# GpSimd's u product in four pieces, VectorE's mixer work in another order, and one down projection whose last k comes at the end

## The reference

```python
# first block: u and vs are gelu of columns of h @ w_in
mixed = einsum('gij,bnjgc->bnigc', masked(sg_w), blocks(layernorm(vs))) + sg_b
sgo = (u * mixed * silu(zs)) @ w_sg_out

# second block: 16 meta rows are put ahead, h has 528 rows
p_pool, p_bval, p_bgate, p_cgate, p_cx = split(rmsnorm(h) @ w_in_2)      # 256 256 256 512 512
y_a = pool_mixer(p_pool)                      # moving means of 2, 4, 8, 16 rows, then a small product
y_b = conformer_conv(p_bval, p_bgate)         # 31-tap causal convolution, layernorm, silu, small product
y_c = gelu(p_cgate) * rglru(p_cx)             # 4-tap convolution, two gates, a linear scan over rows
h = h + concat(y_a, y_b, y_c) @ w_out_2
h = h + square(relu(rmsnorm(h) @ w_up_2)) @ w_down_2
out = rmsnorm(h)[16:]
```

## Time and profile before

| | |
|---|---|
| median of 3 runs | 1053.14 us (1053.1 to 1058.57) |
| profiled execution, its time | 1053.21 us |
| its span | 1051.4 us |
| TensorE busy | 1028.8 us, 98% |
| VectorE, ScalarE, GpSimd busy | 515.1, 421.4, 575.9 us |

### The profile page before, as it was taken

The page is one execution under the profiler, slowest core; times in us unless marked ns, Lnnn a source line. Parts: engine busy times, 40 slices in busy tenths (PEclk is TensorE's granted clock), DMA queues, the critical chain, the costliest instruction groups (busy, mean ns, idle before and its releaser), DMA issues.

```text
span 1051.4 us, 12703 instructions
## 1 busy us (share of the span) xinstructions
PE 1028.8 (98%) x5047; PEld 861.9 (82%) x5047; DVE 515.1 (49%) x835; ACT 421.4 (40%) x663; POOL 575.9 (55%) x712
## 2 busy tenths in 40 slices
PE   9999999999999999999999878999999999999997
PEld 7888888888888888888899766888788888888887
DVE  2781356665356633545677898457113213312323
ACT  5443445555624424443237663453213222212332
POOL 3655556556556764465634796464655544554551
PEclk9999999999999999999999999999999999999999
DMA  6323222122442215332222202322323232232212
GB/s 223 105 92 93 89 70 81 54 67 81 141 140 80 80 45 181 118 120 82 81 80 81 80 21 81 101 81 80 120 80 112 89 110 91 87 113 81 97 64 80
DMA packets 93500, 98.63 MB, mean 94 GB/s; under 512 B 3282, under 2 KB 88816, under 8 KB 93440
## 3 DMA queue, kind: packets, MB, share of 16 engines
q1 hardware_dynamic: 93440, 97.81, 28.7%
HBM read 95.71 MB, written 2.10 MB: 93 GB/s over the span
## 4 chain that ended last, share of the span: by engine, by line
PE 84%; DVE 11%; ACT 4%; issue 1%; DMA 1%; SPq 0%; DVEq 0%; ACTq 0%
PE ps L347 75%; DVE ps L1165 2%; PE ps L714 1%; PE ps L695 1%; PE ps L1623 1%; PE ps L839 1%; DVE Fm L1077 1%; DVE Hl L478 1%; PE ps L652 1%; PE ps L654 1%; DVE tmp L1589 1%; DVE Fm L1129 1%; DMA raw<-in_w_in 1%; DVE tmp L456 1%; DVE Al L1531 1%
## 5 line engine op out<-in xcount | busy, mean ns | idle before, releaser
L268 POOL TENSOR_TENSOR wlo<-raw,whi 128x256 fp32r<-128x256 f32 x668 | 509.4, 794 | 386.1 <-ACT whi L263 386.1
L347 PE MATMUL ps<-Hh,whi 128*128 128x512 f32 x832 | 330.0, 397 | 5.4 <-DVE Hl L1246 1.7
L347 PE MATMUL ps<-Hl,whi 128*128 128x512 f32 x832 | 325.4, 391 | 0.0
L263 ACT ACTIVATE whi<-raw 128x1024 fp32r<-128x1024 f32 x167 | 175.9, 1054 | 159.0 <-PE ps L347 152.7
L347 PE MATMUL ps<-Hh,wlo 128*128 128x512 f32 x832 | 209.1, 390 | 1.0 <-POOL wlo L268 1.0
L347 PE MATMUL ps<-Ah,whi 128*128 128x512 f32 (+1 forms) x576 | 197.7, 366 | 0.2 <-DVE Al L1531 0.2
L347 PE MATMUL ps<-Al,whi 128*128 128x512 f32 (+1 forms) x576 | 195.0, 361 | 0.0
L347 PEld LDWEIGHTS ps<-Hh,whi 128*128 128x128 f32 x832 | 156.9, 189 | 42.7 <-DVE Hl L408 4.2
L347 PEld LDWEIGHTS ps<-Hh,wlo 128*128 128x128 f32 x832 | 156.6, 188 | 34.2 <-POOL wlo L268 1.4
L347 PEld LDWEIGHTS ps<-Hl,whi 128*128 128x128 f32 x832 | 156.9, 189 | 31.8 <-issue 0.5
L347 PE MATMUL ps<-Ah,wlo 128*128 128x512 f32 (+1 forms) x576 | 125.2, 363 | 0.0
(11 more groups left out here) (291 smaller groups left out, 957.2 us busy)
## 6 DMA issues: line engine op xcount, KB each, us to landing
raw<-in_w_in SPq DMA_DIRECT2D x33, 1024.0 KB, 5.3
raw<-in_w_up SPq DMA_DIRECT2D x16, 1024.0 KB, 5.4
raw<-in_w_down SPq DMA_DIRECT2D x16, 1024.0 KB, 5.1
raw<-in_w_att_out SPq DMA_DIRECT2D x4, 1024.0 KB, 5.2
raw<-in_w_sg_out SPq DMA_DIRECT2D x4, 1024.0 KB, 5.2
raw<-in_w_o SPq DMA_DIRECT2D x4, 1024.0 KB, 5.1
raw<-in_w_in SPq DMA_DIRECT2D x6, 512.0 KB, 3.9
Fm<-in_x SPq DMA_DIRECT2D x2, 1024.0 KB, 6.7
```

Source lines behind the costliest of these rows:

```text
L263: eh = A(lambda e, s=s, src=src, kk=kk: e.activation(wtile(whi, s, kk), src, ACT.Copy), raw_ev[b], used)
L268: el = G(lambda e, s=s, src=src, kk=kk, cut=cut: e.tensor_tensor(wtile(wlo, s, kk)[:, *cut], src[:, *cut], f(wtile(whi, s, kk))[:, *cut], ...
L347: return e.matmul(ps[:, bk, 0:c1 - c0], wt, x[:, k, c0:c1], start=st, stop=sp)
```

## The change

1. The u product of each `sg_block` is four GpSimd instructions of two groups of 128 columns instead of one of eight; all are queued together, and the last one signals.
2. `single` takes `tail`, and the first down product of each part gets `tail=1`: the high·high, low·high and high·low matmuls of k 0 to 6 come first, those of k = 7 at the end.
3. In `w_in_2` the two pool products come ahead of the four for `p_cgate`. In each half of `w_out_2` the product over k 0 and 1 comes first: W0, R0, R1, W1, R2, R3.
4. The steps of `mixers` are written anew. The side taps are put one channel at a time (`side_tap`), channel 0's from the fifth step on; the pool mixer comes ahead of the gating; the four gated tiles are handled one at a time, three of them left in their PSUM banks (`at_cg`) until their low half is made; taps stand between a copy's request and its use; `x1_add` comes in two parts behind R0 and R1.

The core of the diff, with the steps that the prediction speaks of:

```diff
+        cols("w_in_2", 0, 0, 1)
         cols("w_in_2", 0, 768, 2)
-        cols("w_in_2", 0, 0, 1)
         for i in range(2):
+            cols("w_out_2", 0, 512 * i, 1, 2, 1)
             cols("w_out_2", 512, 512 * i, 1, 4)
-            cols("w_out_2", 0, 512 * i, 1, 2, 1)
...
-            sg[("u", i)] = G(lambda e: e.tensor_tensor(u, u, t1.rearrange("p (g i) -> p g i", g=8), ALU.mult), e1,
-                             zu_ev[7])
+            t8 = t1.rearrange("p (g i) -> p g i", g=8)
+            for g in range(0, 8, 2):
+                u = F4[:, g:g + 2, 128 * i:128 * i + 128]
+                sg[("u", i)] = G(lambda e, g=g, u=u: e.tensor_tensor(u, u, t8[:, g:g + 2], ALU.mult), e1, zu_ev[7],
+                                 signal=(g == 6))
...
+        def at_cg(c):
+            return ps[:, order4[c], :] if c < 3 else cg[:, c]
...
+                ev = V(lambda e, c=c: e.tensor_tensor(Hl[:, 4 + c], at_cg(c), f(Hh[:, 4 + c]), ALU.subtract),
+                       cg_ev[c])
+                y2[4 + c] = [ev]
+                if c < 3:
+                    bank_free[order4[c]] = ev
...
             cx(3, *made[7])
+            side_tap(0)
             taps(1, (1,))
             rg_conv(3)
             rg_high(3)
+            taps(1, (1,))
             rg_low(3)
+            rg_scan(1)
+            yield
+            rg_gate(2, 0)
+            side_tap(1)
             yield
             rg_gate(2, 1)
+            pool_in(0, *made[8])
+            side_tap(0)
+            rg_input(2)
+            yield
+            rg_gate(3, 0)
+            e3 = pool_mix(0)
+            side_tap(1)
+            yield
+            rg_gate(3, 1)
+            pool_in(1, *made[9])
+            ea = pool_high(0, e3)
+            rg_exps(2)
+            rg_input(3)
+            es = pool_low(0, ea)
+            yield
+            e3 = pool_mix(1)
+            side_tap(1)
+            rg_root(2)
+            table(ACT.Gelu_apprx_tanh)
+            ea = pool_high(1, e3)
+            yield
             scale_cg(0)
+            es1 = pool_low(1, ea)
+            gelus((0,))
...
+            taps(3)
+            side_tap(1)
+            yield
             scale_cg(3)
             gelus((3,))
             taps(1)
+            cg_hi((3,))
             taps(1)
+            cg_lo((3,))
             yield
             taps(3)
             yield
             taps(3)
             yield
+            taps(3)
+            yield
+            x1_add((0, 1), rec_mm)
+            taps(3)
+            yield
+            taps(3)
+            yield
+            x1_add((2, 3), rec_mm)
             taps(N_DVE)
             merged = conv_merge()
...
         for h in range(2):
+            product([[(bk, 0, 512)] for bk in order4], Hh, Hl, y2, (0, 1), 2, last=False, mid=step)
+            step()
             for g in range(2):
-                product([[(order4[2 * g], 0, 512)], [(order4[2 * g + 1], 0, 512)]], Hh, Hl, y2, range(4, 8), 4, last=False, mid=step)
+                rec_mm.extend(product([[(order4[2 * g], 0, 512)], [(order4[2 * g + 1], 0, 512)]], Hh, Hl, y2,
+                                      range(4, 8), 4, first=False, last=(h == 0), mid=step))
                 step()
...
-                bk, em = single(Hh, Hl, acts, nb=nb)
+                bk, em = single(Hh, Hl, acts, nb=nb, tail=1 if n == 0 else 0)
```

More of the change, by code:

```diff
@@ L458, in scaled, with single @@
             return ev
-        def single(xh, xl, kev, ks=range(8), nb=4):
+        def single(xh, xl, kev, ks=range(8), nb=4, tail=0):
             bk = one_bank(nb)
-            return bk, product([[(bk, 0, 512)]], xh, xl, kev, ks)[0]
+            return bk, product([[(bk, 0, 512)]], xh, xl, kev, ks, tail=tail)[0]
         def h_product(nb=4):
@@ L1166, in taps, with side_tap @@
                         acc, ub[:, c, k:k + 512], cw[:, c, k:k + 1], acc, ALU.mult, ALU.add), tap_ev[c])
[L1168 to L1184, removed]
+        def side_tap(c):
+            k = side_at[c]
+            side_at[c] += 1
+            x = ub[:, c, k:k + 512]
+            s, fr = new_tmp()
+            dst = tmp[:, s, 0:512]
+            ea = A(lambda e: e.activation(dst, x, ACT.Copy, scale=cw[:, c, k:k + 1]), ub_ev[c], fr)
+            if k == N_DVE:
+                side_to[c], side_ev[c] = s, ea
+                return
+            acc = tmp[:, side_to[c], 0:512]
+            side_ev[c] = G(lambda e: e.tensor_tensor(acc, acc, dst, ALU.add), ea, side_ev[c])
+            release(s, side_ev[c])
@@ L1250, in conv_merge @@
         def conv_merge():
-            assert tap_at == [N_DVE, N_DVE] and side_at[0] == 31
+            assert tap_at == [N_DVE, N_DVE] and side_at == [31, 31]
             ev, ea = [], []
@@ L1354, in mixers @@
             rg_high(0)
+            taps(1, (0,))
             rg_low(0)
+            side_tap(0)
             yield
             rescale(5, 6)
+            side_tap(0)
             yield
@@ L1360, in mixers @@
             cx(1, *made[3])
-            taps(1, (0,))
+            taps(2, (0,))
             rg_conv(1)
             rg_high(1)
+            taps(1, (0,))
             rg_low(1)
@@ L1374, in mixers @@
             rg_gate(1, 1)
+            taps(2, (0,))
             rg_exps(0)
             rg_input(1)
-            taps(2, (0,))
             yield
             conv_input(1, *made[5])
+            taps(1, (0,))
             rg_root(0)
+            table(ACT.Sigmoid)
             yield
-            side_taps()
+            side_tap(0)
             taps(2, (0,))
             rg_scan(0)
-            table(ACT.Sigmoid)
             yield
             cx(2, *made[6])
-            rg_scan(1)
+            side_tap(0)
@@ L1389, in mixers @@
+            taps(1, (0,))
             rg_conv(2)
             rg_high(2)
+            taps(1, (0,))
             rg_low(2)
             yield
-            side_taps()
-            taps(1, (1,))
+            side_tap(0)
+            side_tap(1)
             yield
             cx(3, *made[7])
-            taps(1)
+            side_tap(0)
+            taps(1, (1,))
+            rg_conv(3)
+            rg_high(3)
+            taps(1, (1,))
+            rg_low(3)
+            rg_scan(1)
             yield
@@ L1421, in mixers @@
+            scale_cg(2)
+            gelus((2,))
             taps(1)
-            yield
[L1423 to L1430, removed]
+            cg_hi((2,))
+            pool_out_low(1, e5)
+            taps(1)
+            cg_lo((2,))
+            side_tap(1)
+            yield
+            taps(3)
+            side_tap(1)
             yield
@@ L1486, in build @@
             step()
+        for i in range(2):
+            made.append(pair_product(mid=step))
+            step()
         order4 = (2, 3, 0, 1) if max(bank_age[0:2]) > max(bank_age[2:4]) else (0, 1, 2, 3)
```

86 lines of the change are left out of this document (29 added, 57 removed).

## The result

The changed kernel takes 1047.07 us (median of six, 1045.33 to 1047.73), the kernel before 1054.86 beside it (six, 1052.78 to 1059.85): a ratio of 0.9915, 95% interval [0.9893, 0.9937]. That is faster, and inside the range. The forecast 1044.9 of 1053.21 is a ratio of 0.9921. The profiled execution took 1047.22, with a span of 1045.3. The kernel before's profiled execution, 1053.21, lies near the short end of its six, so between the two profiled executions the gain is only 6.0 us where 8.3 were forecast, and that the ratio comes so close to the forecast's is in part luck.

A forecast was written before the change was run, and what follows sets the result against it. TensorE, busy for 98% of the span, was taken as the bound, so only its waits could be won: 1053.21 - 6.5 (mixers) - 0.9 (spatial gate) - 0.95 (down product) = 1044.9 us, range 1040 to 1050.5.

The forecast's parts named there:

- The mechanism: Mixers: VectorE's last low half, at 634.2, holds TensorE at R0's seventh matmul; 66 matmuls, 15.0 us, follow to `conv_sums`.
- The mixers' term: Mixers: the new order starts `conv_sums` at 649.2 instead of 655.75, a gain of 6.5 us.
- I let that instruction start where it did: Mixers, VectorE: the third `cx` was assumed to start at 575.75, as in the kernel before.
- GpSimd's idle time: Mixers: channel 0's side-tap additions, four steps earlier, are covered by GpSimd's idle 14.5 of 79.9 us.
- The stretch from there to the last low half: VectorE, third `cx` to last low half: 54.1 us of work plus 4.3 of waits, the latter between 0 and 7.7.
- The gate (2, 1): Mixers: TensorE waits 3 to 4 us for a sigmoid queued behind tile 3's high half, without cost to the end.
- W0 was given some 6: Mixers: TensorE waits some 6 us at W0 for the second pool tile and gated tiles' banks, without cost to the end.
- The small edits: Spatial gate's u product in pieces gains 0.9 us; the first down product's tail gains 0.95 in part 0.
- The waits for ScalarE: Rival, mixers: idle time of 7.7 instead of 4.3 and one more lower-clock stretch give 1049.8 us; chance 0.25.
- The lower clock behind W0's wait: Rival, TensorE at W0: another lower-clock stretch costs 1.5 us, giving 1046.4; inside the forecast's own range, no separate chance.
- VectorE could be faster: Rival, mixers: taps fill every wait and `conv_sums` comes near TensorE's bound of 642.4; about 1040 us, chance 0.18.
- Pieces acting as one: Rival, spatial gate: the u product's four pieces act as one, giving 1045.8 us; inside the forecast's own range, no separate chance.

The follow-up runs named there:

- b4: Changed kernel without GpSimd's additions of the side taps (taps 23 to 30 missing from the convolution): 1043.48 us, one run.
- a4: Changed kernel with all four gated tiles in SBUF, none left in PSUM: 1048.3 us, one run.
- b1: Changed kernel with the high and low halves of recurrence tiles 1 and 3 a step later, so ScalarE has the gates' sigmoids first: 1046.76 us, one run.
- b2: Changed kernel with the second pool tile's high copy moved on ScalarE ahead of the square roots and table load: 1047.82 us, one run.
- b3: Changed kernel with the edits of b1 and b2 together: 1045.23 us, ratio 0.9899 to the kernel before.
- a1: Kernel before with only GpSimd's u product in four pieces: 1053.62 us, one run.
- a2: Kernel before with only the last k at the end of each part's first down product: 1052.07 us, one run.
- a3: Changed kernel with u product in one piece and down products as before, leaving only the new order: 1049.18 us, ratio 0.9933 to the kernel before.
- c1: b3 with each of GpSimd's side-tap additions in two pieces of 256 columns: 1044.5 us, ratio 0.9891 to the kernel before.
- d1: b3 with the second channel half's last four side taps moved behind the last low half: 1044.98 us, ratio 0.9898 to the kernel before.
- d2: b3 with the edits of c1 and d1 together: 1042.58 us, ratio 0.988 to the kernel before.
- e1: d2 with the second pool tile's product and evictions half a product earlier and k = 7 last in R0's first product: 1041.65 us, ratio 0.9856 to the kernel before.

## Why the prediction came out as it did

**The mechanism** was right for the changed kernel. VectorE's last low half sets `conv_sums`: TensorE waits for it at 635.78, and the 66 matmuls behind it take 15.1 us where 15.0 was worked out. When b4 brings it 2.8 us earlier, the sums follow by 2.8, though TensorE then comes 0.1 us behind it and has no wait left. In a4 it is the longer wait at W0, for an earlier low half of the same queue, and the lower clock behind it that hold TensorE.

**The mixers' term was mis-sized**: 4.3 us instead of 6.5. Of the missing 2.2, the step that failed most is "I let that instruction start where it did": the third `cx` comes 1.46 later. The traces show how. TensorE has a new wait of 1.47 us at gate (1, 0), for a sigmoid. From the end of gate (1, 1)'s matmuls, by way of the square roots, to the third `cx` it is 10.31 us in both kernels, so the shift lies ahead of that. On ScalarE that sigmoid stood behind the copy of tile 1's high half and a weight copy before, too, so the order there did not do it. The copy itself is later, because the three instructions of `rg_conv(1)` ahead of it on VectorE are longer. They are, in the kernel before and then in the changed one, with a GpSimd addition beside them:

```profile
555.77 2.69 DVE L1077 SCALAR_TENSOR_TENSOR Fm<-Fm,sm 128x528 f32<-128x528 f32 x3 [0.65 <-ACT Fm L1072]
```

```profile
555.40 3.99 DVE L1079 SCALAR_TENSOR_TENSOR Fm<-Fm,sm 128x528 f32<-128x528 f32 x3
557.07 1.75 POOL L1181 TENSOR_TENSOR tmp<-tmp 128x512 f32<-128x512 f32 x1
```

The addition is one of channel 0's, which the new order moves forward to here; the prediction set these only against GpSimd's idle time. In b4, without additions, the three take 2.79, TensorE's wait there is 0.3, and the third `cx` is 0.27 later than before instead of 1.46. b1 puts the sigmoid ahead of the copy and gains only 0.3, since TensorE then waits 1.1 for the low half of the same late tile.

The stretch from there to the last low half took 59.0 instead of 58.4. The work was 52.2, not 54.1: several instructions with two inputs in SBUF were shorter than before (one scan 1.26 instead of 2.24, the pool mixer's last step 1.21 instead of 1.66). The waits were 6.9, not 4.3. That such errors offset each other fits what b2, b3 and b4 show: where VectorE waits less, it works longer beside GpSimd, and the reverse. They were treated as two independent terms.

**W0 and the gates.** The gate (2, 1) was given 3 to 4 us and has 3.64. W0 was given some 6 and has 1.4, because TensorE was held earlier, by both gates and by the lower clock at 591. As the prediction had it, the waits at W0 and gate (2, 1) cost nothing at the end: b1 shifts the wait from the one place to the other with the same sums within 0.2 us.

**The small edits** were each under by about 0.3: 1.2 us instead of 0.9 and 0.95, alone (a1, a2) as together. Where the other 0.3 lies around the two waits was not traced further.

**The rivals.** The waits for ScalarE are there, but 2.6 us larger than sized, not 3.4, and the work was shorter by 1.9. The lower clock behind W0's wait isn't in this kernel, nor in a3, b2 and b4, where that wait is 1.4 to 1.9 us; it is in a4, b1, b3, c1, d1 and d2, where it is 3.2 to 4.9. The stretch that the changed kernel has at 591 is longer than the one before, 6.7 us instead of 3.3; TensorE waited for the last low half all the same. That VectorE could be faster was right in its work and wrong in its waits. Pieces acting as one is ruled out by L831's 1.65.

## What to carry to other kernels

When an order is rewritten to fill an engine's waits, don't count the waits filled as time won: work put beside GpSimd's gets longer, so count what the neighbour holds (here 6.4 us from additions in 59), and cut the neighbour's instructions or leave operands in PSUM first. Follow a moved copy on its own queue up to the next instruction that another engine waits for, and moved additions to the neighbour's instructions that they lengthen, from the first step that moved, not only in the stretch that seems to matter. Once one deadline is earlier, look at which other wait of TensorE is now the longest: in these traces several waits of 1 us cost less than one of 3 to 5 with a stretch at the lower clock behind it.

## What was not expected of the hardware

- GpSimd's u product takes 4.80 us in four pieces and 3.39 in one, yet VectorE's L831 beside it falls from 3.31 to 1.65.
- A stretch at the lower clock behind `w_o`'s factors is there in some traces and absent in others whose instructions up to that place are the same. It moves what follows by about 1.5 us, so a difference of that size between single profiles of this kernel says nothing about an edit. The same 4 us of the kernel before and of a2_tail, which differs only in the MLP (the clock is the third number from the end):

```profile
530.00:534.00 4.00, 4.00 (x21) 3.67 (x19) 0.99 (x3) 1.70 (x3) 0.00 (x0) 0.57 0.00 0
```

```profile
530.00:534.00 4.00, 4.00 (x29) 3.52 (x29) 1.78 (x8) 1.70 (x3) 0.92 (x2) 1.00 0.00 0
```

- Several waits of about 1 us (4.6 us in all in e1 from 575 on) left the clock at 1.00 up to 649; a single one of 3.2 (d2) or 3.6 us (after) went with 0.50. One of 2.2 at a gate went without in the kernel before and in a2, and with 0.50 at 592 in a1. The Trainium skill, "TensorE: Matmul & The Clock Gate", section "HAM oscillation — how this bites in real kernels", says that a burst behind a long wait starts at the lower clock. Waits of 1.5 us, which the prediction held against it, are no test of that. The long waits here agree; the stretch at 530 does not: what stands ahead of it are one-column matmuls without a gap over 0.3 us.
